# Recurrence stage: POOL makes the rates in buffers of their own ahead of the exponentials, and DVE's work for the next chunk is placed in other levels

## The reference, cut to what matters

```python
def wkv_scan(state, r, w, a, b, k, v, reverse):
    def step(S, inp):
        r_t, w_t, a_t, b_t, k_t, v_t = inp
        sa = jnp.einsum('bhvk,bhk->bhv', S, a_t)
        S = S * w_t[:, :, None, :] + sa[..., None] * b_t[:, :, None, :] + v_t[..., None] * k_t[:, :, None, :]
        return S, jnp.einsum('bhvk,bhk->bhv', S, r_t)
    ...
for d in range(N_DIR):
    rev = d == 1
    s0 = jnp.zeros((B, RWKV_HEADS, RWKV_HEAD, RWKV_HEAD), jnp.float32)
    s_ctx, yc = wkv_scan(s0, *rwkv_scan_inputs(fc, d), reverse=rev)
    _, yx = wkv_scan(s_ctx, *rwkv_scan_inputs(fx, d), reverse=rev)
```

## Time and profile before

| what | value |
|---|---|
| median of 3 runs | 2823.26 us (2822.31 to 2835.34) |
| profiled execution, its own time | 2821.54 us |
| its span, first to last instruction | 2819.4 us |
| mean granted TensorE clock | 0.932 |
| busy share PE, DVE, ACT, POOL | 86%, 43%, 28%, 14% |
| recurrence of layer 0 | about 562 to 793 us of the span |
| recurrence of layer 1 | about 2042 to 2275 us |

### The profile page before, as it was taken

How to read it: one execution, slowest core, us unless ns; L and a number is a source line. 1 busy time by engine, 2 the same in 40 slices (tenths; PEclk the granted TensorE clock), 3 DMA queues, 4 the chain that set the end, 5 groups by cost and what they waited for, 6 DMA issues and landing times. The chain is left out here.

```text
span 2819.4 us, 53869 instructions
## 1 busy us (share of the span) xinstructions
...
## 2 busy tenths in 40 slices
...
GB/s 351 221 226 191 137 25 30 53 4 5 4 131 152 83 0 64 239 393 352 344 347 243 335 90 89 90 30 92 61 3 4 4 211 81 188 396 354 378 355 199
DMA packets 75779, 462.25 MB, mean 164 GB/s; under 512 B 19088, under 2 KB 28432, under 8 KB 46480
## 3 DMA queue, kind: packets, MB, share of 16 engines
...
## 5 line engine op out<-in xcount | busy, mean ns | idle before, releaser
L508 PE MATMUL win_ps<-h,win_ring 128*128 128x512 f32 (+1 forms) x1024 | 397.2, 549 | 13.6 <-PEq L2670 8.2
L2314 PE MATMUL xp_psG<-moe_ring,rt_xt 128*64 128x256 f32 (+1 forms) x2048 | 349.9, 394 | 1.1 <-DMA moe_ring<-in_moe 0.8
L508 PEld LDWEIGHTS win_ps<-h,win_ring 128*128 128x128 f32 x1024 | 195.7, 192 | 205.9 <-issue 199.3
L2314 PEld LDWEIGHTS xp_psG<-moe_ring,rt_xt 128*64 128x64 f32 (+1 forms) x2048 | 254.1, 166 | 71.7 <-issue 14.2
L568 DVE SCALAR_TENSOR_TENSOR mod_acc<-ada_ring,cv_silu,mod_acc 128x512 f32<-128x512 f32 x280 | 198.0, 748 | 10.8 <-issue 0.4
L2335 PE MATMUL xp_psY<-moe_ring,rt_aT 128*64 128x512 f32 (+1 forms) x512 | 178.9, 606 | 12.8 <-DVE rt_aT L2587 12.8
L1930 PE MATMUL mg_psG<-h,mg_ring 128*128 128x512 f32 (+1 forms) x480 | 166.7, 507 | 0.0
L2195 POOL DMA_INDIRECT y_rows<-rt_y,rt_dst x92 | 92.4, 1004 | 485.2 <-PE xp_psT L2299 249.0
L2580 DVE TENSOR_TENSOR rt_sg<-rt_sg,xp_psG 128x128 f32<-128x128 f32 x92 | 26.4, 288 | 282.7 <-ACT rt_sg L2386 282.7
L2299 PEld LDWEIGHTS xp_psT<-cst,rt_xg 128*128 128x128 f32 x736 | 84.9, 144 | 107.6 <-DMA rt_xg<-h_rows,rt_tok 68.1
L2592 DVE COPY rt_y<-xp_psY 128x512 f32<-128x512 f32 x92 | 63.6, 692 | 181.0 <-DMA y_rows<-rt_y,rt_dst 115.9
...
## 6 DMA issues: line engine op xcount, KB each, us to landing
moe_ring<-in_moe SPq DMA_DIRECT2D x128, 1536.0 KB, 10.8
...
```

Source lines behind the costliest of these rows:

```text
L508: last = pe.matmul(ps[:, n % NB, first(n):T], ring[:, j % 2, c, m * P:(m + 1) * P], h[:, c, first(n):T], start=c == 0, stop=c == KD - 1)
L2314: last = pe.matmul(psG[at:at + m, u % 2, 0:2 * P].rearrange("p (q n) -> p q n", q=2), xt[:, u % 2, c, at:at + m], ring[:, slot, c:2 * KD:K ...
```

## The change

POOL gets a function `rates` that makes `bb` and `kd` without a wait, into buffers of their own; `operands` is left with the two products with `sc_ex`. POOL does this for chunk 0 too, which DVE did before. DVE's and ACT's work for the next chunk is put into other levels: the masks of the levels come in two pieces (plane 2, then planes 3 to 5), sums of d = 0 and 1 stand in m = 1 and 3, queries in m = 2 and 4; on ACT the exponentials stand in m = 1 and 3 and the `tok` copies in m = 2 and 4. `cmask` counts three pieces a chunk, and PE waits for the third ahead of m = 3.

```diff
@@ -1388,7 +1388,7 @@
 
     names = ("gates", "exps", "feats", "queries", "mats", "turned", "masked", "parts", "tok", "cmask", "x", "xi", "nn", "nout",
              "ntout", "rhs", "rhsout", "u", "uout", "sy", "yout", "state")
-    per_step = dict(gates=1, exps=1, feats=1, queries=1, mats=1, turned=1, masked=1, parts=1, tok=1, cmask=2, x=6, xi=6, nn=5,
+    per_step = dict(gates=1, exps=1, feats=1, queries=1, mats=1, turned=1, masked=1, parts=1, tok=1, cmask=3, x=6, xi=6, nn=5,
                     nout=4, ntout=5, rhs=1, rhsout=1, u=1, uout=1, sy=1, yout=1, state=1)
     sem = [dict(zip(names, k.signals(*[f"scan{d}_{n}" for n in names]))) for d in range(2)]
     (bonus_done,) = k.signals("scan_bonus")
@@ -1409,7 +1409,9 @@
         vst = sb("vst", [P, KC, L])
         ex = sb("ex", [P, 3, KC, L])
 
-        bb, kd, S2 = E, R, Z
+        bb = sb("bb", [P, KC, L])
+        kd = sb("kd", [P, KC, L])
+        S2 = Z
 
         ra = [sb("ra", [P, KC, 2, L]),
               [pn[:, NK_T + d].rearrange("p (c a n) -> p c a n", c=KC, a=2) for d in range(2)]]
@@ -1487,10 +1489,10 @@
                             if m < 5:
                                 act.activation(N[d][:], psN[d], ACT.Copy).then_inc(sem[d]["nout"].sem, 1)
                             act.activation(NT[d][:], psNT[d], ACT.Copy).then_inc(sem[d]["ntout"].sem, 1)
-                        if m <= 2 and n + 1 < NST:
-                            exponentials(m - 1, n + 1)
-                        if m in (3, 4):
-                            d = m - 3
+                        if m in (1, 3) and n + 1 < NST:
+                            exponentials(m // 2, n + 1)
+                        if m in (2, 4):
+                            d = m // 2 - 1
 
                             w(act, d, "turned", n)
                             act.activation(bk[d][:, 0:HEADS:2], psBK[d][0], ACT.Copy)
@@ -1519,17 +1521,20 @@
                     step(n)
                 act.wait_ge(bonus_done.sem, bonus_done.at(1))
 
-            def operands(eng, d, n):
+            def rates(pool, d, n):
 
                 col = columns(d, n)
-                w(eng, d, "exps", n)
-                eng.tensor_tensor(bb[d][:], kk[:, :, col], aa[:, d, :, col], ALU.mult)
-                eng.tensor_tensor(kd[d][:], ka[:, :, col], aa[:, d, :, col], ALU.mult)
-                eng.drain()
-                eng.tensor_tensor(kd[d][:], kd[d][:], pr[:, K_T:K_T + KC, col], ALU.add)
-                eng.drain()
-                eng.tensor_tensor(hat[d][:, :, 0], bb[d][:], ex[d][:, 2], ALU.mult)
-                eng.tensor_tensor(hat[d][:, :, 1], kd[d][:], ex[d][:, 2], ALU.mult).then_inc(sem[d]["feats"].sem, 1)
+                pool.tensor_tensor(bb[d][:], kk[:, :, col], aa[:, d, :, col], ALU.mult)
+                pool.tensor_tensor(kd[d][:], ka[:, :, col], aa[:, d, :, col], ALU.mult)
+                pool.drain()
+                pool.tensor_tensor(kd[d][:], kd[d][:], pr[:, K_T:K_T + KC, col], ALU.add)
+                pool.drain()
+
+            def operands(pool, d, n):
+
+                w(pool, d, "exps", n)
+                pool.tensor_tensor(hat[d][:, :, 0], bb[d][:], ex[d][:, 2], ALU.mult)
+                pool.tensor_tensor(hat[d][:, :, 1], kd[d][:], ex[d][:, 2], ALU.mult).then_inc(sem[d]["feats"].sem, 1)
 
             def queries(dve, d, n):
 
@@ -1541,9 +1546,12 @@
 
             @block.gpsimd
             def _(pool):
-                for n in range(1, NST):
+                for n in range(NST):
+                    for d in range(2):
+                        rates(pool, d, n)
                     for d in range(2):
                         operands(pool, d, n)
+                    pool.drain()
 
                 for d in range(2):
                     w(pool, d, "mats", NST - 1)
@@ -1621,16 +1629,20 @@
                     for d in range(2):
                         correct(d, 1)
                     for d in range(2):
-                        levels(d, 2, 6).then_inc(sem[d]["cmask"].sem, 1)
+                        levels(d, 2, 3).then_inc(sem[d]["cmask"].sem, 1)
                     for m in range(1, 6):
                         for d in range(2):
                             if m > 1:
                                 correct(d, m)
-                        if m <= 2 and n + 1 < NST:
-                            w(dve, m - 1, "turned", n)
-                            cumulate(m - 1, n + 1)
-                        if m in (3, 4) and n + 1 < NST:
-                            queries(dve, m - 3, n + 1)
+                        if m == 2:
+                            for d in range(2):
+                                levels(d, 3, 6).then_inc(sem[d]["cmask"].sem, 1)
+                        if m in (1, 3) and n + 1 < NST:
+                            d = m // 2
+                            w(dve, d, "turned", n)
+                            cumulate(d, n + 1)
+                        if m in (2, 4) and n + 1 < NST:
+                            queries(dve, m // 2 - 1, n + 1)
                     for d in range(2):
                         w(dve, d, "rhs", n)
                         dve.tensor_copy(rhs[d][:], psR[d])
@@ -1652,7 +1664,6 @@
                     cumulate(d, 0)
                 for d in range(2):
                     queries(dve, d, 0)
-                    operands(dve, d, 0)
                 for d in range(2):
                     first_levels(d, 0)
                     masks(d, 0)
@@ -1689,8 +1700,8 @@
                                 w(pe, d, "masked", n)
                             elif m > 1:
                                 w(pe, d, "nout", n, m - 1)
-                                if m == 2:
-                                    w(pe, d, "cmask", n, 2)
+                                if m <= 3:
+                                    w(pe, d, "cmask", n, m)
                             else:
                                 w(pe, d, "xi", n, 1)
                             for h, hp, r in heads:
```

## The result

| what | before | after |
|---|---|---|
| median of 19 runs each, us | 2827.39 (2822.31 to 2835.34) | 2837.61 (2824.68 to 2846.82) |
| ratio | 1 | 1.004, 95% interval 1.0029 to 1.005 |
| profiled execution, own time and span, us | 2821.54, 2819.4 | 2841.76, 2839.2 |
| mean granted TensorE clock | 0.932 | 0.929 |
| busy share PE, DVE, ACT, POOL | 86%, 43%, 28%, 14% | 86%, 43%, 28%, 15% |

The changed kernel is slower by 0.4%, some 11 us, and the whole interval lies above 1. The two profiled executions are 20 us apart. The one of before is faster than each of the 19 timed runs of before, the one of after is 4 us above its median, so the pair shows the places of the loss, but its size less well.

A forecast was written before the change was run, and what follows sets the result against it. PE and DVE, both nearly full, were taken to bound the chunk in turns. 14 chunks x 1.3 + 0.8 = 19.0 us on the profiled 2821.54, plus 1.7 to the median, gave 2842 us; 8-in-10 range 2824 to 2852.

The forecast's parts named there:

- the 0.8 for chunk 7: Chunk 7 of layer 1: level 1's masks now stand in level 2 beside the bonus, +0.8 us (bounds 0 to 2).
- slower by over 0.5%: Outcome class for the whole time, joining the forecast's own case (0.56) and the slower-by-more case (0.11); chance 0.67.
- the middle class: Outcome class for the whole time: within 0.5% of before; chance 0.26.
- no change: Rival: POOL and DVE don't collide in level 2; -0.3 to +0.4 us a chunk, 2819 to 2829 us; chance 0.26.
- Level 1: First level of a chunk: smaller masks all hidden, level 2 gains 0.04 us, more than 1.2 us of room unused.
- Level 2: Masks of planes 3 to 5 and queries, 2.41 us against room of 1.73, plus POOL's turns of 1.10: level 3 +0.63.
- Level 3: Sums of d = 1 take 2.17 us, 2.84 with the XI pair against PE's 2.40: level 4 begins +1.07.
- Level 4: DVE idles 0.6 us for the exponentials, then queries beside POOL take 1.77: first XI of level 5 +1.5, 1.3 a chunk.
- PE's waits: Named sign in layer 0: PE's wait for XI grows from 9.4 us to some 18, else the prediction is wrong.
- Chunk 0: First chunk of a layer: DVE rid of ten operations, POOL's rates beside its sums; 0, bounds -1.5 to +1.5 us a layer.
- Faster: Rival: smaller pieces let PE run at its pace through all levels; 1.75 us a chunk or 24 us, 2799; chance 0.07.
- Slower by more: Rival: rates collide with the first masks too and PE's pauses add; 2.1 us a chunk, 2853; chance 0.11.

The follow-up runs named there:

- e4: Changed kernel with POOL's two products behind the exponentials done for only 2 of 64 tokens; ratio 0.9985 against before.
- e3: Changed kernel with the masks of planes 2 to 5 back in one piece in level 1; ratio 0.9982 against before.
- e1: Kernel before with POOL's half alone (rates ahead in own buffers, chunk 0 on POOL), DVE's and ACT's order as before; ratio 0.999.
- e2: Kernel before with only the new order on DVE and ACT, POOL still making all five operations behind the exponentials; ratio 1.006.
- e5: Changed kernel with masks of planes 2 to 4 in level 1, plane 5 in level 2, queries in levels 4 and 5; ratio 0.9976 against before.

## Why the prediction was right in its way and too high in its size

The time of 2837.61 lies in the range, 4.4 below the forecast of 2842. The mechanism was as forecast, and two sizes were off that went against each other. The base of the sum was 2823.26, the median of three runs, where 19 runs give 2827.39; and the loss was 19.0 in the sum, where the medians differ by 10.2. On the better base the same sum would have said 2846, 9 too many, so that the forecast came within 4.4 us was in part luck. Of the 19.0 the profiles show 13.3: fourteen chunks at 1.3 were 5.2 too much against 0.93, and the 0.8 for chunk 7 was not there. The rest up to 10.2 is in the difference between these two profiles and the medians. The largest chance, 0.67, stood on slower by over 0.5%. The measured 0.4% is in the middle class, which had 0.26, though it is not the "no change" that this class was made from: the interval excludes 1.

**Level 1, right.** Forecast: all hidden, XI of level 2 at 6.1, over 1.2 us of room unused. Measured 6.06 in chunk 1 (6.19 in the median), with 1.09 idle.

**Level 2, right, and the step on which it all rests.** Forecast: second mask 1.4 to 1.5, two turns of 0.55, level 3 at 10.6. Measured 1.48, a query at 0.94, level 3 at 10.58 (10.52). e4 takes POOL's products away and with them 1.04 us where the sum had 1.10. e3 takes the masks away and restores the time, e1 and e2 show that it is this half of the change. The Trainium skill's rule on the shared ports (SBUF — State Buffer, SBUF: two separate sides), which the prediction weighed against the change, is borne out by that.

**Level 3, right.** Sums of 2.16 (617.22 to 619.38), forecast 2.17, level 4 at 13.41, forecast 13.5. No other placing tried here removed this overrun; it stands in e5 too.

**Level 4, the term that was mis-sized.** The prediction took 1.77 for the queries beside POOL, as at 617.34 of before, and so 1.3 a chunk. Here DVE's first query began at 620.65, 0.05 ahead of POOL's product, and went through at 0.42; only the second waited, 0.95. From the first query to XI are 621.87 - 620.65 = 1.22, one turn and not two. So it was in seven of the twelve chunks. In the other five POOL's product came first, the first query lasted 0.70 to 0.92, and 1.49 to 1.72 went by to XI. Level 5 came at 15.90 in chunk 1 instead of 16.5, and 0.97 later than before in the median, so 0.9 a chunk. Both wait for the same `sc_ex`; who comes first decides whether there are one or two turns, and the prediction had "start together" and paid for the worse case in every chunk. All five are chunks in which the clock fell, and in them PE let the second XI of level 4 begin only 0.46 to 0.86 behind the first. Idle time ahead of them was 0.53, forecast 0.6.

**PE's waits, wrong.** The text said that the wait for XI would grow from 9.4 us to some 18, and that the prediction was wrong if it did not. It fell to 6.2. What it overlooked is the wait that the change itself adds: x of level 3 waits for the third `cmask`. The text had that piece at 613.5, "ahead of XI's own delay: nothing further". The instant was right (615.43 after the change, 9.46 behind the chunk's first `sc_N`, as 613.5 is 9.44 behind its own), and in this kernel so was the cost, since DVE was busy with the queries until 616.55 anyway. But PE stood at the mask first, so a part of DVE's lateness shows as waits for `sc_cm` and `pr`, 7.2 us in layer 0, where before it was 0.2. The three together are 13.4 against 9.6 before. They grew by 3.8, less than the 8.6 forecast. The smaller term of level 4 takes some 2.8 of that off (0.4 in each of seven chunks); and the seven chunks grew by 5.9, so even the sum of these waits doesn't hold the whole loss. Part of the rest is PE's busy time where its clock fell, 24.39 us in chunk 5 against 22.86 in chunk 1. The named sign was thus the wrong row for a right mechanism.

**Chunk 0, within its bounds in layer 0 alone, and the ends.** Forecast 0, bounds of 1.5 either way: +0.41 in layer 0. POOL's rates beside DVE's sums did slow them, as said. In layer 1 the pause of 8.99 us moved from the levels of chunk 0 (33.26 to 28.91, 4.35 less) to its start (6.51 more), 2.2 us on balance, outside the bounds. The prediction had not looked at layer 1 and had no term for it. Chunk 7 of layer 1 was to cost 0.8; its stretch became 0.12 shorter. In layer 0 the block still ended with the bonus, and the stretch was 0.76 shorter, where 0 was forecast.

**The chunks, added up.** Seven chunks of 1.3 were 9.1 us in a layer. In layer 0 the seven stretches grew by 0.47 + 6 x 0.91 = 5.9.

**The rivals.** "No change" needed no collision in level 2, and there was one. "Faster" needed each piece within 1.73 us of room. The changed kernel doesn't have that, but e5 comes nearer and is faster by 0.24%, not by the 0.9% that rival gave. The sums of d = 1 still overrun, by the rows; whether that is all of the gap stays open. The Trainium skill's rule that breaking up instructions may let work be completed sooner (Perfetto Trace Analysis, Optimizing Scalar/DVE Operations) did not hold for the pieces as placed here, 1.004. Whether it holds in another placing is open: e5, with the masks in pieces, is at 0.9976, but e3, with the masks in one piece, is at 0.9982, and the two can't be told apart. "Slower by more" needed the rates to collide with the first masks: one rate began at 626.67 and took 1.09, but the masks there kept 0.69 and 0.68.
